# A gather of expert rows with nine row buffers in place of twelve, and the weight ring left to the weights

## What is computed

```python
# PEER: for each of 256 tokens, 8 heads x 16 experts = 128 experts out of 16384
q = (hx @ w_q)                      # keys are scored, 16 + 16 best of each head, then 16 best of 256 sums
expert = (i1 * N_KEYS + i2)         # 128 indices for each token
u_sel = u[expert]; v_sel = v[expert]            # rows of 1024 floats each
act = gelu(einsum('nd,ned->ne', hx, u_sel))
out = einsum('ne,ned->nd', gate * act, v_sel)
# then, four times in the rest of the model (the first stands right behind PEER):
h = h + 0.5 * (silu(n @ w_gate) * (n @ w_up)) @ w_down     # d_ff = 2816
```

## Time and profile before

| | us |
|---|---|
| median of three runs | 2249.59 |
| the profiled execution | 2247.54 |
| its span in the trace | 2245.6 |

### The profile page before, as it was taken

The page is one execution under the profiler, slowest core; times in us unless marked ns, Lnnn a source line. Parts: engine busy times, 40 slices in busy tenths (PEclk is TensorE's granted clock), DMA queues, the critical chain, the costliest instruction groups (busy, mean ns, idle before and its releaser), DMA issues. The chain is left out here.

```text
span 2245.6 us, 24222 instructions
## 1 busy us (share of the span) xinstructions
PE 1842.1 (82%) x9222; PEld 1363.7 (61%) x9222; DVE 1452.2 (65%) x2709; ACT 549.8 (24%) x701; POOL 400.1 (18%) x342
## 2 busy tenths in 40 slices
PE   3798868777787777879996556999999999549999
PEld 2576553333333333359996445599989987436998
DVE  7883359888878888567765985155555554634554
ACT  1123011000001000034442000154444433123442
POOL 0020025444453544400000453000000000000000
PEclk9899989899998989999998787999999999769999
DMA  8471358999999999935543111534535453203543
GB/s 358 155 281 59 129 230 365 421 421 421 421 422 421 412 422 415 421 118 184 205 160 121 38 57 38 187 130 179 196 141 190 178 183 132 94 0 141 192 175 128
DMA packets 63850, 502.07 MB, mean 224 GB/s; under 512 B 7200, under 2 KB 7456, under 8 KB 11296
## 3 DMA queue, kind: packets, MB, share of 16 engines
q0 software_dynamic: 37008, 268.98, 29.0%
q1 hardware_dynamic: 25776, 229.40, 28.1%
q10 hardware_dynamic: 992, 2.74, 0.3%
HBM read 500.04 MB, written 1.05 MB: 223 GB/s over the span
## 5 line engine op out<-in xcount | busy, mean ns | idle before, releaser
L739 PE MATMUL PB<-arena 128*128 128x512 f32 x604 | 303.2, 660 | 112.1 <-DVE arena L1313 112.1
L755 PE MATMUL PB<-h_lo,gu_hi 128*128 128x256 f32 x1344 | 382.1, 284 | 0.0
L755 PE MATMUL PB<-h_hi,gu_hi 128*128 128x256 f32 x1344 | 375.1, 279 | 4.8 <-DVE gu_lo L1334 4.8
L755 PE MATMUL PB<-h_hi,gu_lo 128*128 128x256 f32 x1344 | 375.6, 279 | 0.0
L1867 POOL DMA_INDIRECT arena<-in_uv,eidx x193 | 226.5, 1174 | 428.6 <-PE PB L739 218.4
L739 PEld LDWEIGHTS PB<-arena 128*128 128x128 f32 x604 | 124.2, 211 | 290.6 <-issue 148.0
L1305 DVE CUSTOM_DVE_ANT_0 arena<-arena,XN 128x1024 f32<-128x1024 f32 x193 | 230.6, 1221 | 76.6 <-DMA arena<-in_uv,eidx 76.6
L755 PEld LDWEIGHTS PB<-h_hi,gu_hi 128*128 128x128 f32 x1344 | 252.6, 188 | 8.8 <-DVE gu_lo L1334 5.7
L755 PEld LDWEIGHTS PB<-h_lo,gu_hi 128*128 128x128 f32 x1344 | 252.6, 188 | 3.1
L755 PEld LDWEIGHTS PB<-h_hi,gu_lo 128*128 128x128 f32 x1344 | 252.4, 188 | 0.0
L1334 DVE TENSOR_TENSOR gu_lo<-ring,gu_hi 128x2048 fp32r<-128x2048 f32 x85 | 194.9, 2293 | 74.3 <-ACT gu_hi L1745 73.7
(11 more groups left out here) (336 smaller groups left out, 2993.2 us busy)
## 6 DMA issues: line engine op xcount, KB each, us to landing
ring<-in_ffn SPq DMA_DIRECT2D x88, 1536.0 KB, 6.5
arena<-in_ada SPq DMA_DIRECT2D x23, 768.0 KB, 6.5
ring<-in_qkv SPq DMA_DIRECT2D x12, 1024.0 KB, 4.8
ring<-in_zg SPq DMA_DIRECT2D x8, 1024.0 KB, 8.6
ring<-in_s5b SPq DMA_DIRECT2D x8, 1024.0 KB, 4.8
ring<-in_ada SPq DMA_DIRECT2D x4, 1536.0 KB, 13.7
ring<-in_up SPq DMA_DIRECT2D x4, 1024.0 KB, 4.9
ring<-in_wo SPq DMA_DIRECT2D x4, 1024.0 KB, 4.9
```

What stands on the lines that cost most here:

```text
L739: mm = pe.matmul(PB[2 + 2 * t + h][:, :], lhsT=diag(n), rhs=uv[n % UVB][:, 1, h * 512:(h + 1) * 512], start=False, stop=False, skip_group_ ...
L755: mm = pe.matmul(PB[j % 2][:, b * T:(b + 1) * T], lhsT=w[:, j % 2, o:o + P], rhs=h[:, k, :], start=(k == 0 and m == 0), stop=(k == DC - 1 ...
```

## The change

`UVB` becomes 9. The three buffers in the ring go, so rows 9 and on wait for the row nine before, not twelve before. The two buffers on the key tables become number 7 and 8, and the wait for the key scores moves from row 10 to row 7. `load_ffn` loses its special case: all four ring slots are filled for the first feed-forward block as soon as the four units of the PEER query weights are used, ahead of the gather and beside its first rows, and no load stands behind line 398 any more.

```diff
-UVB = 12
+UVB = 9
@@
-        ring_tail = ring[:, 2:4, :].rearrange("p a b -> p (a b)")
         uv = ([part(16384 + 2048 * j, 2, D) for j in range(6)] + [part(1024, 2, D)]
-              + [ring_tail[:, 2048 * j:2048 * (j + 1)].rearrange("p (a b) -> p a b", b=D) for j in range(3)]
               + [part(4096 + 2048 * j, 2, D) for j in range(2)])
@@ def load_ffn(f):
-                first = 0
-
                 def one(j, row):
                     ...
-                if f == 0:
-                    sp.wait_ge(unit_done, u0 - NS + 1)
-                    one(0, 0)
-                    sp.wait_ge(uv_used, TT * NSLOT)
-                    first = 1
-                rounds = (FU - first) // NS
+                rounds = FU // NS
                 with sp.Fori(0, rounds) as i:
-                    for j in range(first, first + NS):
+                    for j in range(NS):
                         sp.wait_ge(unit_done, i * NS + (u0 + j - NS + 1))
                         one(j, i * (NS * P) + (f * FU + j) * P)
-                for j in range(first + rounds * NS, FU):
+                for j in range(rounds * NS, FU):
@@ the gather's issues, on GpSimd
                     elif n == 6:
                         pool.wait_ge(h2_ready, TT)
                     elif n == 7:
-                        pool.wait_ge(unit_done, UNIT[("pq", 2)] + 1)
-                    elif n == 10:
                         pool.wait_ge(sc_full, PH)
```

## The result

| | before | after |
|---|---|---|
| median, us | 2250.95 | 2287.72 |
| span of the profiled execution | 2245.6 | 2286.3 |
| ratio, 95% interval | | 1.0164 (1.0146 to 1.0181) |

The change costs 37 us in this comparison, where 15.5 were forecast; the time lies above the range. Over all executions the kernel before took between 2246.1 and 2257.2 us, the changed one between 2275.5 and 2290.7, so the loss itself is clear and its size is known to some 10 us.

A forecast was written before the change was run, and what follows sets the result against it. The prediction took DMA transfers to bound the gather; 7.5 us for the first fill plus 8 us for the steady state made 15.5 us, 2265 us on the median, with a range of 2254 to 2284.

The forecast's parts named there:

- What bounds: In the gather of 256 rows, DMA transfers at 421 GB/s set the time, 2.49 us a row.
- Part 1: At the gather's start, three rows fewer are issued before the first buffer is released; cost 7.5 us.
- Part 2: In the gather's steady loop, DMA engines run dry behind slow groups beside routing step 3; cost 8 us, bounds 0 and 21.
- W + 9.2: Latest issue of the next row in the gather without loss, in us after W, when a group's last row lands.
- W + 10.1: Issue seen in the gather beside a routing step 3 with slow first matmuls on TensorE, taken as 0.9 us late.
- The second reading: Late in the gather, rates falling from 421 to 416 and 418 GB/s were taken to give 5.3 us for 14 groups.
- W + 14.9: Latest landing of the second row two groups on in the gather that keeps the DMA engines from stopping.
- Part 3: Loads of units 1 to 3 moved beside the gather's first rows: cost 0, gain between 0 and 1.3 us, taken as 0.
- Part 4: Small edits, such as the key-score wait moved from row 10 to row 7 and SyncE's dropped wait: 0 us.
- Too thin everywhere: Rival: in the gather a short queue costs another 1 us per burst; 2283, or 2291 with all steps; chance 0.15.
- Not slower: Rival: one engine's 8 us lag at the gather's end vanishes with nine buffers, so time is 2249; chance 0.07.
- step 3: The routing step beside 14 of the gather's groups, where VectorE writes diagonals late; about one in two was predicted slow.

The follow-up runs named there:

- e10: The kernel before, twelve buffers, with a reordered start: first four dots and the second head's routing before the wait for ScalarE's first exponential; 2239.49 us, ratio 0.9946.
- e6: The kernel before with all twelve buffers, but row 9 waits until row 0 is used; 2258.97 us, ratio 1.0035.
- e1: The changed kernel's nine buffers, but the loads of units 1 to 3 stay behind the gather as in the kernel before; 2282.17 and 2287.29 us.
- e7: The changed kernel with the diagonals of every group written before its piece of routing; 2259.01 us, ratio 1.0030.
- e4: The changed kernel with four matmuls of zeros on TensorE ahead of each group beside routing step 3; 2280.73 us, ratio 1.0146.
- e5: The changed kernel with the diagonals written before the routing only in groups beside routing step 3; 2283.49 us, ratio 1.0143.
- e9: The changed kernel with eight buffers, one more taken away; 2355.85 us, ratio 1.0458.

## Why the prediction was wrong, point by point

- **What bounds.** Right: the transfers set the end of the gather, and the 7.5 us and later the 11 us of e10 came through in full.
- **Part 1, the first fill, 7.5 us.** Right: row 9 goes out where row 12 did, 44.4 us after row 0, and e6 shows the price alone, 8 us.
- **Part 2, the steady state, 8 us.** The mechanism was right and the size was not: the loop loses 22 to 32 us in the four traces of nine buffers with the late release (changed kernel and e1, twice each). The step that failed is the limit "W + 9.2". It took the least latency of a row that meets an idle queue, 5.7 us, as what a row needs to follow the one before without a gap. The landings say that a loss begins at W + 7.5, so by the prediction's own W + 14.9 a row needs some 7.4 us. The groups that the prediction counted as "in time", W + 8.3 and W + 8.4, therefore lose about 0.6 us each, those at W + 8.5 to 9 about 1.1, and there are many of them, beside all steps. The late ones at W + 10.1 lose 2.5 us, not 0.9. The share of late ones, half of 14, was nearly right: 8 or 9 of 14 in five traces came later than W + 9.5.
- **The second reading**, 416 and 418 GB/s late in the gather, gave 5.3 us and seemed to confirm the sum. It looked at the engines that run ahead of the slowest. The first of them needs only 5.0 us at least from issue to landing, not 5.7, and what such an engine loses costs the kernel before nothing: around 800 us the lead of the fast engines falls from 8.2 to 6.6 us, while the landings keep their pace. That the 5.3 us came near the first sum was chance.
- **Part 3, the loads.** Right for the cost (nothing, under 25 us of idle time) and for the gain (20.3 against 20.0 us to unit 1's split).
- **Part 4.** Right for the changed kernel: the fill takes the same time, so the moved wait holds nobody there.
- **The rivals.** "Too thin everywhere" named 2283, with "another 1 us per burst" as its price, and came nearest, in kind too: behind a short queue a row does take longer than its least latency. It had the loss start only in the slow groups, though, and e7 shows that with the release early enough nine buffers lose nothing. "Not slower" had one half right: the lag of the one engine did shrink with the shorter queue, from 8 us to about 1.5. It gave nothing back, for the end was set by that engine in both kernels: in the kernel before too its landings are held up by about 1 us in every 20 to 24 rows (3.43 to 3.51 us between two landings in place of 2.49), which makes 2.53 us a row on average. With the short queue the other engines can't run ahead of these hold-ups any more. The minus 8 us that this rival put on it was wrong.
- **The range** took 1 us a burst as the worst. With W + 7.5 in place of W + 9.2 the prediction's own working gives 7 late groups x 2.5 + 7 others of step 3 x 0.7 + some 20 of steps 0 to 2 beyond W + 7.5, x 0.6 = 34 us beside the fill, 2292 on the median. This is an estimate after the event, for the loss per group is taken from the table above; it counts the single hold-ups that the kernel before has too, and so comes out high against the 22 to 32 measured.

## What to carry to other kernels

In a loop in which a transfer may start only when a buffer is released, take for each kind of iteration the latest release, not the average, and ask that the next request goes out a good margin (here 1.7 us) before the least latency would demand. Where buffers are short, release them first and do side work behind: moving the diagonals ahead of the routing was worth 20 to 29 us with nine buffers, nearly as much as the tenth buffer. Before buffers are traded for early loads, ask whether anyone waits for these loads; here nobody did.

## What the runs showed of the hardware that I had not expected

- A queue that still holds a row is not enough to keep the DMA engines busy. I took the landings in five traces with nine and eight buffers (after, e1_nine_old_loads, e4, e5, e9), from row 14 on, by how long before the landing of the row ahead a row's issue instruction had ended. With 4.5 us or more a row took 2.52 us on average, with 3.5 to 4.5 us 2.70, with 2.5 to 3.5 us 3.18, with 1.5 to 2.5 us 3.24, with less 3.71, and when the row ahead had already landed 5.30. A row that meets an empty queue lands 4.46 us at least after its issue instruction has ended, of which 2.48 are its own; by that alone 2.0 us ahead should be enough, and the full pace needs twice that. What the engines do in the 2 us between, no run shows.
- GpSimd's issue of a row takes 0.93 us at least and up to 1.96 in the changed kernel, with no change in the instruction, and what it takes more delays the landing by as much: the least time from its end to the landing is 4.46 us where it took 0.94 and 4.50 where it took 1.85. Which work beside it makes it long was not tried apart.
- One DMA engine is held up by about 1 us once in 20 to 24 rows (rows 86, 107, 131, 151, 171, 195, 215 and 242 of the kernel before). With twelve buffers the others run on, and its lag grows from 0.5 us to 8 us in 400 us and then stays between 6.5 and 8.5. With nine buffers it stays near 1.5 us in the changed kernel (at most 2.7) and near 2.5 in e7 (at most 3.6). The pace of the gather is that of this engine in e7 as in the kernel before, 2.53 us a row. Why it is held up, no run shows.
